# Expert weights: gate and up loaded ahead of down, and one table for expert and flag, in a mixture-of-experts stage

## What is computed

```python
def hier_moe(h, lw):                      # h: 1152 tokens of 1024 values
    g_idx = jnp.argmax(g_logits, axis=-1)              # one of 4 groups for a token
    top_l, top_i = lax.top_k(e_sel, TOP_K_IN_GROUP)    # 2 of its 4 experts
    weights = p_g * jax.nn.softmax(top_l, axis=-1)
    expert_ids = g_idx[:, None] * EXPERTS_PER_GROUP + top_i
    combine = jnp.sum(jax.nn.one_hot(expert_ids, N_EXPERTS, dtype=jnp.float32) * weights[..., None], axis=1)
    hidden = (jax.nn.silu(jnp.einsum('nd,edf->nef', hf, lw['w_exp_gate']))
              * jnp.einsum('nd,edf->nef', hf, lw['w_exp_up']))
    y = jnp.einsum('nef,efd->nd', hidden * combine.astype(hf.dtype)[..., None], lw['w_exp_down'])
```

## Time and profile before

| | |
|---|---|
| runs of the kernel | 1496.74, 1498.19 (median), 1499.64 us |
| profiled execution, its time | 1498.28 us |
| its span, first to last instruction | 1496.4 us |
| mean granted TensorE clock | 0.885 of full speed |
| TensorE matmuls busy | 1147.0 us, 77% of the span |
| VectorE, ScalarE, GpSimd busy | 39%, 29%, 15% |
| expert stage, first product of gate and up to the last step's transpose | 895.84 to 1427.19 us |

### The profile page before, as it was taken

The page is one execution under the profiler, slowest core; times in us unless marked ns, Lnnn a source line. Parts: engine busy times, 40 slices in busy tenths (PEclk is TensorE's granted clock), DMA queues, the critical chain, the costliest instruction groups (busy, mean ns, idle before and its releaser), DMA issues. The chain is left out here.

```text
span 1496.4 us, 19567 instructions
## 1 busy us (share of the span) xinstructions
PE 1147.0 (77%) x7006; PEld 803.9 (54%) x7006; DVE 580.8 (39%) x1031; ACT 428.5 (29%) x853; POOL 229.0 (15%) x163
## 2 busy tenths in 40 slices
PE   4999999899998789897999847446356656556575
PEld 1787777689987788886888742112112212112132
DVE  1745451156578677775566521001001000001028
ACT  3631111243376566666465101000000000000012
POOL 0000000200067357772000010000000000000031
PEclk8999999999999899998999868768778777868788
DMA  9436774211081542312432382352471252423165
GB/s 342 156 140 236 236 250 129 66 37 29 1 197 51 124 117 71 89 57 59 145 123 85 113 292 79 123 182 84 133 262 57 87 183 97 130 96 99 57 228 222
DMA packets 126846, 196.88 MB, mean 132 GB/s; under 512 B 19504, under 2 KB 92112, under 8 KB 124702
## 3 DMA queue, kind: packets, MB, share of 16 engines
q1 hardware_dynamic: 116108, 162.22, 34.2%
q0 software_dynamic: 5760, 20.97, 4.2%
q10 hardware_dynamic: 4882, 12.44, 2.2%
HBM read 382.85 MB, written 39.24 MB: 282 GB/s over the span
## 5 line engine op out<-in xcount | busy, mean ns | idle before, releaser
L2151 PE MATMUL moe_gu_ps<-moe_wgu,moe_xT 128*32 128x512 f32 x1408 | 210.0, 751 | 225.2 <-DMA moe_wgu<-in_w_exp_up 224.6
L2151 PEld LDWEIGHTS moe_gu_ps<-moe_wgu,moe_xT 128*32 128x32 f32 x1408 | 53.3, 134 | 363.3 <-issue 362.4
L2252 DVE COPY moe_hidT<-moe_h_ps 128x256 f32<-128x256 f32 x22 | 9.3, 424 | 335.8 <-PE moe_h_ps L2160 335.8
L2198 ACT COPY moe_xT<-moe_x_ps 128x512 f32<-128x512 f32 x22 | 12.9, 587 | 390.8 <-PE moe_x_ps L2137 390.8
L96 PE MATMUL proj_acc_ps<-proj_w_hi,hidden_hT_hi 128*128 128x512 f32 x288 | 117.1, 407 | 7.5 <-DVE hidden_hT_lo L91 7.5
L98 PE MATMUL proj_acc_ps<-proj_w_hi,hidden_hT_lo 128*128 128x512 f32 x288 | 114.6, 398 | 0.0
L97 PE MATMUL proj_acc_ps<-proj_w_lo,hidden_hT_hi 128*128 128x512 f32 x288 | 114.1, 396 | 0.0
L1322 POOL TENSOR_TENSOR att_e<-att_e 128x1152 f32<-128x1152 f32 (+1 forms) x36 | 86.0, 2390 | 73.3 <-DVE att_e L1402 73.3
L1340 ACT ACTIVATE att_e<-att_sc_ps,att_shift 128x1152 f32<-128x1152 f32 (+1 forms) x72 | 81.5, 1132 | 41.2 <-DVE att_shift L1391 41.1
L2124 POOL DMA_INDIRECT moe_xg<-scratch_h,all_step_token x22 | 20.8, 947 | 451.8 <-PE moe_x_ps L2137 414.3
L1391 DVE TENSOR_REDUCE att_shift<-att_sc_ps 128x1 f32<-128x1152 f32 (+1 forms) x72 | 86.2, 1230 | 5.4 <-PE att_sc_ps L1436 5.3
(11 more groups left out here) (372 smaller groups left out, 2112.7 us busy)
## 6 DMA issues: line engine op xcount, KB each, us to landing
moe_wgu<-in_w_exp_gate SPq DMA_DIRECT2D x178, 512.0 KB
moe_wgu<-in_w_exp_up SPq DMA_DIRECT2D x178, 512.0 KB
moe_wd<-in_w_exp_down SPq DMA_DIRECT2D x89, 1024.0 KB
scratch_y_slots<-moe_y ACTq DMA_DIRECT2D x22, 512.0 KB, 3.5
proj_raw<-in_w_in SPq DMA_DIRECT2D x32, 256.0 KB, 4.9
proj_feat<-in_w_ada SPq DMA_DIRECT2D x4, 2048.0 KB, 8.1
proj_xh<-in_w_ada SPq DMA_DIRECT2D x4, 2048.0 KB, 9.7
proj_feat<-in_w_ada SPq DMA_DIRECT2D x4, 1024.0 KB, 5.7
```

Source lines behind the costliest of these rows:

```text
L2151: mm = pe.matmul(gu_ps[n % 2][at, :], xT[:, n % 2, k * P + c * Q:k * P + (c + 1) * Q], wgu[:, c, k], start=(k == 0), stop=(k == KT - 1))
L2198: act.copy(xT[:, n % 2, left], x_ps[:, left]).then_inc(x_left, 1)
L2252: dve.tensor_copy(hidT[:], h_ps[:, 0:FF]).then_inc(hidT_done, 1)
```

## The change

SP's loop is shifted. In turn n it now issues gate and up of step n and behind them down of step n - 1, for which it waits until down(n - 2) is done. It has one turn more, and in its first there is no down, in its last no gate and up. Each entry of the one table `block_weights` holds the expert and, times 16, the flag; SP takes them apart with register operations. The table entries of a step are read at the start of its turn, which is now ahead of the loads of down of the step before. In the routing stage the flag now decides in all four columns over the first loads (in columns 1 to 3 it is always set).

```diff
-def expert_of(eng, W, c, step):
+def weights_of(eng, W, c, step):
     n = c * STEPS + step
-    return eng.value_load(W["block_expert"][0:1, n:n + 1], min_val=0, max_val=NE - 1)
-def is_new(eng, W, c, step):
-    n = c * STEPS + step
-    return eng.value_load(W["block_new"][0:1, n:n + 1], min_val=0, max_val=1)
+    code = eng.value_load(W["block_weights"][0:1, n:n + 1], min_val=0, max_val=2 * NE - 1)
+    return code & (NE - 1), code >= NE
...
             sp.wait_ge(blocks_done, 1)
-            firsts = [expert_of(sp, W, c, 0) for c in range(STREAMS)]
-            other = is_new(sp, W, 0, 0)
+            firsts = [weights_of(sp, W, c, 0) for c in range(STREAMS)]
             for half in range(2):
                 sp.wait_ge(W["gu_in"][half], 16 * 2)
-                load_gate_up(sp, I, W, 0, half, firsts[0], cond=other)
-                for c in range(1, STREAMS):
-                    load_gate_up(sp, I, W, c, half, firsts[c])
+                for c, (e, new) in enumerate(firsts):
+                    load_gate_up(sp, I, W, c, half, e, cond=new)
...
-            dve.tensor_copy(W["block_expert"][0:1, :], of_block[:].rearrange("p c s -> p (c s)"))
-            dve.tensor_scalar(fresh[:, :, 0:1], of_block[:, :, 0:1], 0.0, None, ALU.not_equal)
+            dve.tensor_scalar(fresh[:, 0:1, 0:1], of_block[:, 0:1, 0:1], 0.0, None, ALU.not_equal)
+            dve.tensor_scalar(fresh[:, 1:, 0:1], of_block[:, 1:, 0:1], 0.0, None, ALU.is_ge)
             dve.tensor_tensor(fresh[:, :, 1:], of_block[:, :, 1:], of_block[:, :, 0:STEPS - 1], ALU.not_equal)
             dve.drain()
-            dve.tensor_copy(W["block_new"][0:1, :], fresh[:].rearrange("p c s -> p (c s)")).then_inc(blocks_done, 1)
+            dve.scalar_tensor_tensor(out=W["block_weights"][0:1, :], in0=fresh[:].rearrange("p c s -> p (c s)"), scalar=float(NE),
+                                     in1=of_block[:].rearrange("p c s -> p (c s)"), op0=ALU.mult, op1=ALU.add).then_inc(blocks_done, 1)
...
-            for n in range(1, STEPS):
-                experts = [expert_of(sp, W, c, n) for c in range(STREAMS)]
-                new = [is_new(sp, W, c, n) for c in range(STREAMS)]
+            ahead = []
+            for n in range(1, STEPS + 1):
+                now, ahead = ahead, [weights_of(sp, W, c, n) for c in range(STREAMS)] if n < STEPS else []
                 for half in range(2):
                     sp.wait_ge(gu_done[half], n)
-                    for c in range(STREAMS):
-                        load_gate_up(sp, I, W, c, half, experts[c], cond=new[c])
-                sp.wait_ge(d_done, n)
-                for c in range(STREAMS):
-                    load_down(sp, I, W, c, experts[c], cond=new[c])
-            for half in range(2):
-                sp.wait_ge(gu_done[half], STEPS)
+                    for c, (e, new) in enumerate(ahead):
+                        load_gate_up(sp, I, W, c, half, e, cond=new)
+                if now:
+                    sp.wait_ge(d_done, n - 1)
+                for c, (e, new) in enumerate(now):
+                    load_down(sp, I, W, c, e, cond=new)
             load_final_gains(sp, I, W, M)
```

More of the change, by code:

```diff
@@ L1913, in _ @@
             sp.wait_ge(blocks_done, 1)
-            firsts = [expert_of(sp, W, c, 0) for c in range(STREAMS)]
-            other = is_new(sp, W, 0, 0)
+            firsts = [weights_of(sp, W, c, 0) for c in range(STREAMS)]
             for half in range(2):
                 sp.wait_ge(W["gu_in"][half], 16 * 2)
-                load_gate_up(sp, I, W, 0, half, firsts[0], cond=other)
-                for c in range(1, STREAMS):
-                    load_gate_up(sp, I, W, c, half, firsts[c])
+                for c, (e, new) in enumerate(firsts):
+                    load_gate_up(sp, I, W, c, half, e, cond=new)
             sp.wait_ge(W["d_in"], 16)
-            load_down(sp, I, W, 0, firsts[0], cond=other)
-            for c in range(1, STREAMS):
-                load_down(sp, I, W, c, firsts[c])
+            for c, (e, new) in enumerate(firsts):
+                load_down(sp, I, W, c, e, cond=new)
         @block.gpsimd
@@ L2447, in build @@
             mixer_stage(nc, I, C, W, M)
-        W["block_expert"], W["block_new"] = s.sb("block_expert", [P, BLOCKS], I32), s.sb("block_new", [P, BLOCKS], I32)
+        W["block_weights"] = s.sb("block_weights", [1, BLOCKS], I32)
         W["step_token"], W["step_weight"] = s.sb("step_token", [P, STEPS], U32), s.sb("step_weight", [P, STEPS])
```

## The result

The changed kernel takes **1268.8 us** (median of 4 runs, 1268.32 to 1269.35) against 1498.7 us of the kernel before in the same comparison: the ratio is 0.8468, with a 95% interval of 0.8453 to 0.8482. The forecast was 1261 us, in a range of 1246 to 1289. The profiled execution has a span of 1266.5 us against 1496.4, so 229.9 us less where the sum said 237.0. One execution of `tables_sooner` in experiment 7 took 2802 us; it was disturbed and is left out of that median.

The account below looks back on a forecast made before the run. SP's issue order, gate and up behind down and table reads, made TensorE and DMA take turns. Waits and lower clock -277.4, given back +41, tables -0.6: -237.0 from 1498.2, so 1261 us, range 1246 to 1289.

Parts of the forecast that it names:

- What bounds the kernel: Expert stage: gate and up loads issued behind down and table reads; at most 277.4 us can go, leaving 244.3.
- Quiet steps: The 12 of 21 steps without an expert change: skipped loads cost nothing, SP's 7.5 us fits under 11.68.
- Changing steps: The nine steps where one or more columns change expert: late loads give back 41 us in all.
- Step 8: All four columns change: both halves of gate and up and down late, work behind them slow, 29.6 us together.
- Step 13: Two columns change: first half 3.0 us late and slow, second not late, down 2.3 late; 9.4 us together.
- single changes: Seven steps where one column changes: late by 0.5 or 1.1 us in three of them, 2 us in all.
- Outside the stage: Before and after the expert stage: -0.6 us in routing from one table read fewer, nothing at the end.
- Transfers do bound a step: Rival, chance 0.17: transfers bound every changing step, all seven single changes late and slow; 1289 us.
- The four table reads: Rival, chance 0.08: remaining reads take 5.2 us, nine changing steps lose 2.3 us each, 21 us; 1282 us.
- The clock rival: Rival, chance 0.06: without gaps the expert stage gets 0.89 of the clock, 244 us become 274; 1291 us.
- The one on the other side: Rival, chance 0.01: slower than before, if down's skipped loads wait behind real ones, 31 us in each of nine steps.
- The better case: Rival, chance 0.10: gather costs nothing (1250 us) and the four-column change moves at 383 GB/s (1245 us).

Follow-up runs that it names:

- tables_sooner: Changed kernel with gathers held later, down loaded in halves, and the next table entries read ahead of the wait for down: 1266.2 us, ratio 0.8446.
- experiment 7: Changed kernel run again unedited: 1266.2 us, ratio 0.8447; beside it tables_sooner, also 1266.2 us.
- experiment 3: Changed kernel with the expert-change flag 0 behind the first step, so all later expert loads are skipped: 1224.2 us (one run).
- experiment 1: Shifted order alone, with the two old tables and eight reads a turn, against the kernel before: 1286.6 us, ratio 0.8575.
- experiments 1 to 5: Edits of order, tables, flags, gather and down's loads, on the kernel before or the changed one: from 1452.1 us (table alone) to 1224.2 us (no expert changes).
- experiment 6: Changed kernel with one column's expert loaded in every step: 1315.5 us, ratio 0.8780; with two columns: 1421.5 us (one run).
- column0_always: Changed kernel with column 0's flag set in every step, so its expert is always loaded again: 1315.5 us, ratio 0.8780.
- down_halves: Changed kernel with down's weights loaded and waited for in two halves of columns: 1268.8 us, ratio 0.8458.

## Why the prediction was right, and where it was off

**What bounds the kernel** held: the wait was SP's order, and the bound of 244.3 us for a stage without it was measured at 244.5 (experiment 3). **Quiet steps** cost nothing, with four reads and even with eight (experiment 1), as SP's 7.5 or 10.1 us lie under 11.68.

**Changing steps.** The periods from one transpose of hidden to the next give what each lost above 11.68 us. Step 8 lost 28.8 us (29.6 in the sum), in its three parts: 10.25 and 1.9 slow, 4.14 and 1.5 slow, 7.72 and 2.9 slow. The parts held to about 1 us each, some too high and some too low. The first half landed 1001.22 - 983.14 = 18.1 us behind its first issue, where the sum had 17.0. Step 13 lost 10.1 (9.4), but not as worked out. Its first half was 3.03 late as said and ran at full speed, so the second half was 2.06 late, where I had 0; down was 2.88 late and then 1.7 slow. That the total agrees is luck. In the second trace of the same code (experiment 7) the first half did run slow, the second had no wait, and the step lost 9.9 us:

```profile
1079.42 5.34 PE L2145 MATMUL moe_gu_ps<-moe_wgu,moe_xT 128*32 128x512 f32 x32 [3.19 <-DMA moe_wgu<-in_w_exp_up]
...
1086.13 3.64 PE L2145 MATMUL moe_gu_ps<-moe_wgu,moe_xT 128*32 128x512 f32 x32
```

The same code gave both, so it does not decide which of the two happens.

The seven **single changes lost 6.1 us, where the sum has 2**: steps 3 (1.8), 4 (0.9), 5 (0.7), 18 (2.6) and 19 (0.1). This is the term that was mis-sized, in two places. Where TensorE had to wait, one expert landed 7.57, 7.31, 8.33 and 8.05 us behind its first issue (steps 3, 4, 5, 18) instead of 5.8 + 1.4 = 7.2; and SP issued it 0.3 us later than in the sum, and in step 18 1.2 us later, at 1141.15 - 1134.94 = 6.2 us instead of 5.0 us after the start of the half before. In step 18 SP's and TensorE's rows are

```profile
1141.15 0.38 SPq L1853 DMA_DIRECT2D moe_wgu<-in_w_exp_gate  x1
```

```profile
1149.20 1.07 PE L2145 MATMUL moe_gu_ps<-moe_wgu,moe_xT 128*32 128x512 f32 x8 [2.40 <-DMA moe_wgu<-in_w_exp_up]
```

which is 8.05 us for one expert. Without the gather it landed within 5.65 (real load issued at 1133.81, TensorE going on at 1139.46 without a wait). So the gather cost at least 2.4 us there, and not 1.4. In step 3 one expert took 930.74 - 923.17 = 7.57 us and still 7.32 without the gather. So the gather cost 0.25 us there. What makes that one slower than the 5.98 that it took in the kernel before stays open; without the gather the DMA engines were busy only 65% of 922 to 930 us, so it was not that they were full, and no run moved the store of y.

**Outside the stage** I had -0.6 us for the routing stage and 0 for the end. The start of gate_up(1, 0) moved by +0.1 and what follows the stage grew by 2.0 us (71.2 against 69.2). Neither is shown to be the change's: the same code gave 67.8 in experiment 7, and starts of the variants of experiments 1 to 5 lie between 902.6 and 909.1. So no run shows the 0.6 us of the routing stage. The sum of the misses is 45.3 - 41 = 4.3 in the stage, 0.7 ahead and 2.0 behind: 7.0 of the 7.1 us between 237.0 and 229.9.

**The rivals.** Transfers do bound a step once the loads follow one another without rest (experiment 6), but in this routing only steps 8 and 13 were so dense; single changes were late by 2.4 us at most, and the halves behind them were not slow. The four table reads that the change took away stand in the way only at real loads, for 18 us (I had priced 21). The clock rival is refuted by experiment 3. The one on the other side, a skipped load that waits behind real ones, would show as waits for skipped loads; only changing steps have waits, each for a load that is real. The better case, 1242 to 1252, did not come: the gather was not free, and step 8 cost as much as in the sum although the DMA engines moved 374 to 385 GB/s from 990 to 1012 us. **The page against the row:** by the Trainium skill ("DMA: Bandwidth & Descriptors", the anatomy of one DMA) the estimate was 1246 us; the kernel took 1268.8, so the rows' landing times were the better guide. The page's fit is for one DMA issued by GpSimd; a half of gate and up is eight loads issued by SP.

## What to carry to other kernels

Issue loads from an in-order queue in the order in which their buffers come free, not in the order in which one step uses them: a single wait placed too early held gate and up behind down here. It put SP's register reads on the path in 20 of 21 steps, and in the nine in which an expert changed the whole transfer too. Cost such a change from the work that each load gains above it (7 to 8 us here) against its landing time beside all other transfers of those microseconds, not its landing time alone. Once the queue is off the path, a shorter issue is worth far less: 47 us of table reads became 18, and moving a transfer from one full stretch to another gave nothing that could be measured.

## What the runs showed of the hardware

- A skipped load took SP 0.07 us, the first real one of a half 0.38 us, and TensorE went on 0.2 us after the last skipped one (925.01 and 925.20). Real loads that follow one another take SP longer: in step 8 of the changed kernel up to 2.40 us each.
- Reading one value of a table in SBUF into SP's register, with the register operations behind it, took 0.65 us (eight in 5.2 us).
- With two columns loaded in every step the DMA engines moved 384 GB/s over 445 us. With one column it was 346 GB/s at a DMA share of 0.98. The Trainium skill ("DMA: Bandwidth & Descriptors", Specifications) puts one core's share of HBM at about 358 GB/s. The traces do not agree: with this one core at work, before the first store of y, while only weights and tokens were loaded, the kernel before moved 383 GB/s over 19 us, and 410 GB/s in the stretch from 890 to 895 us.
- After waits of 2.25 to 3.40 us TensorE's next work ran at either level of its clock. The changed kernel went on at 2.4 GHz after 3.03 us (3.64 us for the half) and at 1.2 GHz for part of the work after 2.88 us (5.34 us), and `column0_always` had 5.34 us behind a wait of 2.70. After the waits of 2.40 us and less in the changed kernel it stayed up. But in `down_halves` a half behind a wait of 2.25 us took 5.24 us, and in `column0_always` one behind 3.40 us took 3.64. So the length of the wait alone does not decide it.
